# Another order for the attention's last seven tiles: 7, 0, 5, 1, 4, 2, 3 instead of 7, 5, 4, 3, 2, 1, 0

## The chip, the core and the metric

The kernel runs on one core of a Trainium2 chip. The metric is the device time of one execution in microseconds (us), the median over several runs. A core has a matrix engine (TensorE, PE in the profile), a vector engine (VectorE, DVE), an activation engine (ScalarE, ACT), a general engine (GpSimd, POOL) and a queue engine for transfers (SyncE, SP). Each runs its own instructions in order; they wait for one another through semaphores.

## The reference

The program is one inference step of a two-layer decoder trunk. Layer 0 mixes tokens by sparse attention, layer 1 by a recurrent block, and an expert mixer follows each. The change lies in layer 0's attention over the prompt of 2048 tokens:

```python
def block(args):                       # one block of Q_BLOCK = 128 queries
    qb, qib, wib, start = args
    q_pos = start + jnp.arange(Q_BLOCK)
    sc = indexer_scores(qib, wib, ki, q_pos, k_pos)     # causal
    _, idx = lax.top_k(sc, topk)                        # topk = 256
    valid = idx <= q_pos[None, :, None]
    return sparse_attend(qb, gather_rows(k, idx), gather_rows(v, idx), valid)
...
out = lax.map(block, (to_blocks(q), to_blocks(qi), to_blocks(wi), jnp.arange(nblk) * Q_BLOCK))
```

The 16 blocks don't depend on each other. There are 16 query heads and 4 key/value heads of 64 columns. The result goes through `attn_w_out`, is scaled by a gate and added to the input.

## The kernel before, in words

`phase_attend` (from L783) works through 16 **tiles** of 128 queries. Tile t sees the first 128(t + 1) keys, so its work grows with t. `TILE` (L848) lists the order; here "place m" is a position in that list and "tile t" the block of queries. The kernel doesn't gather keys. It computes all scores and hides those that were not chosen with a mask (`hide`). For tiles below `NPRE` = 9 the mask was made in an earlier phase and is loaded; for tiles 9 to 15 the indexer's work and the search run inside this phase.

All engines walk through the same stages: stage i works on the scores and values of place i and prepares the next places beside that. A stage has 2(t + 1) **slots** (`slots`, half of `S`), and `middle` is half of them. What a stage does in its slots:

- every slot: PE adds the mask and the maxima into two banks of PSUM (L1315), adds the scores by keys (L1322), and multiplies the two exponentials of the slot before by the values (L1333); ACT takes the exponentials (L1074);
- **first half** (slots below `middle`): the row maxima of the *next* place. PE fills a pair of scratch banks `aux` with scores in bf16 (L1342, `fill`), DVE takes the row maximum of each bank (L1166, `largest`). One pair of fills with its two maxima is a "pair" below; a next tile of up to 512 keys has 8 pairs, one of 513 to 1024 keys 16, of which every second covers the keys beyond 512. `fill` waits until the maximum that used the same bank is done. `unit_pairs_at` spreads the pairs evenly over the slots of the first half;
- first half too: DVE divides the *previous* place's output by its totals (`normalise`: four reciprocals at L1180 and one product at L1183), spread by `normal_at`, but all at once in slot 1 if `middle` is 2 or less;
- slot `middle`, after its own scores and values: PE projects the previous place's output (L1354, 32 matmuls), once the maxima of the next place (`maxed`) and the normalising (`o_normed`) are done;
- then ACT copies the projection (L1093) and the first half of this place's output (L1084), PE transposes the queries of place i + 2 (L1392), ACT copies them (L1120), and POOL adds the residual (L1040, L1043), sends it off (L1046) and narrows those queries to bf16 (L1051), which the next stage's `fill` needs.

So stages of neighbouring tiles are coupled: the number of pairs comes from the next tile, and the number of slots into which they go from this one:

```python
def unit_pairs_at(i, s):
    return share_of(U[i + 1] // 2, s, 0, max(middle(i), 1)) if there(i + 1) else range(0)
...
def normal_at(i, s):
    if middle(i) <= 2:
        return range(5) if s == min(1, middle(i)) else range(0)
    return share_of(5, s, 1, middle(i))
```

On PE a slot's order is: scores of this slot, the first half of its pairs, the values of the slot before, the other half of its pairs, and in slot `middle` the projection. When the last place is done, the phase ends with a barrier of all engines, and the sample group's phases follow.

Of the kernel before, what the change touches and what calls it, by code (L numbers as in the profile page):

```python
# [30 lines left out]
NT = SEQ // P  # L31
# [239 lines left out]
NPRE = 9  # L271
# [511 lines left out]
def phase_attend(nc, T):  # L783
# [7 lines left out]
    with ExitStack() as ctx, Semaphores(nc, T["whole_run"], ("y_out",)) as sems:  # L791
# [53 lines left out]
        hide_in = [sem("hide_in0"), sem("hide_in1")]  # L845

        RAMP = [6, 8]
        TILE = RAMP + [t for t in range(NT - 1, -1, -1) if t not in RAMP]  # L848
        L = [P * (t + 1) for t in TILE]
        CUTS = [-(-l // 512) for l in L]  # L850
        U = [H * c for c in CUTS]
        I = [0 if t < NPRE else IH * c for t, c in zip(TILE, CUTS)]
        S = [NKV * (t + 1) for t in TILE]
        PIECES = 37
# [5 lines left out]
        def there(m):  # L860
            return 0 <= m < NT

        def early(m):

            return there(m) and TILE[m] < NPRE

        def late(m):
            return there(m) and TILE[m] >= NPRE

# [97 lines left out]
        def rows_at(m):  # L967
            return slice(TILE[m] * P, TILE[m] * P + P)

# [2602 lines left out]
def build(nc, T):  # L3572
    with ExitStack() as stack:
# [8 lines left out]
        with ExitStack() as attention:  # L3582

            keep("KT", [P, NKV // 2, SEQ], until=attention)
            keep("kiT", [P, SEQ], until=attention)
            keep("V1", [P, NT, NKV, P], until=attention)
            with ExitStack() as projecting:
                keep("project_w", [P, KC, C_END], until=projecting)
                phase_modulation(nc, T)
                phase_project(nc, T)  # L3590
            phase_attend(nc, T)
# [81 lines left out]
```

## Time and profile before

| | us |
|---|---|
| median of 3 runs (5066.58 to 5074.35) | 5068.48 |
| the profiled execution: its time | 5068.78 |
| the profiled execution: its span | 5067.0 |
| PE busy, of the span | 4355.4 (86%) |
| DVE busy | 2225.7 (44%) |
| ACT busy | 1889.3 (37%) |
| POOL busy | 589.8 (12%) |

The span is what the profiler saw from the first instruction to the last; the time is 1.8 us more. The phase of the change runs from about 750 to 2480 us of it, its last seven tiles from 2076 us on.

### The profile page before, as it was taken

To read this page: it belongs to the slowest core of one execution; us is meant where nothing else is said; L and a number is where in the kernel's file an instruction comes from. 1 tells how busy PE (TensorE), PEld (TensorE's weight loads), DVE (VectorE), ACT (ScalarE), POOL (GpSimd) and SP (SyncE) were. 2 spreads that over 40 slices of the span, in tenths; PEclk is the share of its full clock that TensorE was granted. 3 is DMA by queue.
4 is the path that set the end of the run, shared out by engine and by line. 5 is a ranking of instruction groups with operands and counts; after the bars stand their busy time and mean duration, and the time that the engine had idled before them with its cause. 6 is when DMAs were issued, how large, how long until landed. Compare 5 with 4: busy or idle time off the path is not lost. (4 is left out here: it accounts for less than half of the span.)

```text
span 5067.0 us, 52791 instructions
## 1 busy us (share of the span) xinstructions
PE 4355.4 (86%) x15065; PEld 2214.0 (44%) x15067; DVE 2225.7 (44%) x5697; ACT 1889.3 (37%) x3264; POOL 589.8 (12%) x742
## 2 busy tenths in 40 slices
PE   7998876789999999998586699997999997699990
PEld 1544431223333333433334344444677775444440
DVE  1167875555655654233354211114566665411116
ACT  0134424766766663333122122222444443122223
POOL 0111111001011100112212000001000001100002
PEclk9999996889999999999886899997999998799995
DMA  8111111000000000000455777754121113467777
GB/s 303 51 50 45 38 37 53 11 7 15 9 15 15 13 15 15 28 27 21 155 179 218 296 278 282 264 195 149 52 71 67 67 38 123 154 237 284 285 263 283
DMA packets 152352, 596.45 MB, mean 118 GB/s; under 512 B 24303, under 2 KB 28271, under 8 KB 133176
## 3 DMA queue, kind: packets, MB, share of 16 engines
q1 hardware_dynamic: 99894, 424.39, 23.4%
q0 software_dynamic: 34208, 119.30, 6.8%
q10 hardware_dynamic: 18036, 50.22, 2.5%
q8 instruction: 97, 1.59, 0.1%
q14 instruction: 117, 0.96, 0.1%
HBM read 457.85 MB, written 136.06 MB: 117 GB/s over the span
## 5 line engine op out<-in xcount | busy, mean ns | idle before, releaser
L2728 PE MATMUL experts_ps_gu<-w_sb,experts_xT 128*128 x1504 | 679.3, 605 | 42.1 <-DMA w_sb<-moe_w_in 37.5
L1333 PE MATMUL attend_po<-attend_PT,V 128*128 128x512 f32 x1088 | 562.3, 638 | 23.5 <-ACT attend_total L1084 23.5
L763 PE MATMUL project_pj<-project_w,project_hT 128*128 128x424 f32 (+1 forms) x1360 | 510.7, 530 | 1.1 <-ACT project_hT L496 1.1
L3456 PE MATMUL recurrent_psAB<-recurrent_hT,rec_w_in_sb 128*128 128x256 f32 x2048 | 469.3, 383 | 0.8 <-ACT recurrent_hT L3122 0.8
L2728 PEld LDWEIGHTS experts_ps_gu<-w_sb,experts_xT 128*128 128x128 f32 x1504 | 285.0, 195 | 371.4 <-issue 371.4
L3456 PEld LDWEIGHTS recurrent_psAB<-recurrent_hT,rec_w_in_sb 128*128 128x128 f32 x2048 | 391.3, 192 | 68.8 <-issue 17.1
L1074 ACT ACTIVATE attend_PT<-attend_big 128x512 f32<-128x512 f32 x544 | 293.8, 592 | 329.8 <-PE attend_big L1322 328.9
L1111 ACT ACTIVATE attend_passed<-attend_score,attend_cand 128x2048 bf16<-128x2048 f32 (+6 forms) x217 | 365.5, 1684 | 100.5 <-DVE attend_cand L1224 82.5
L1166 DVE CUSTOM_DVE_ANT_0 attend_junk<-attend_aux,attend_hide 128x512 bf16<-128x512 f32 (+3 forms) x512 | 297.6, 620 | 195.4 <-issue 118.4
L2682 DVE SCALAR_TENSOR_TENSOR experts_th<-experts_th,experts_ps_gu 128x256 f32<-128x256 f32 x94 | 39.6, 422 | 747.1 <-ACT experts_th L2661 747.1
L763 PEld LDWEIGHTS project_pj<-project_w,project_hT 128*128 128x128 f32 (+1 forms) x1360 | 248.5, 187 | 245.0 <-issue 236.2
L2718 PE MATMUL experts_ps_y<-w_sb,experts_midT 128*128 x752 | 342.2, 598 | 11.5 <-issue 11.5
L1333 PEld LDWEIGHTS attend_po<-attend_PT,V 128*128 128x128 f32 x1088 | 188.2, 194 | 311.1 <-issue 248.9
L1322 PE MATMUL attend_big<-attend_qT,KT 64*128 64x512 f32 x1088 | 320.6, 667 | 0.0
L2661 ACT ACTIVATE experts_th<-experts_ps_gu 128x256 f32<-128x256 f32 x94 | 36.0, 383 | 677.9 <-PE experts_ps_gu L2728 677.9
L1342 PE MATMUL attend_aux<-attend_KTb,attend_qTb 64*128 64x512 bf16 (+3 forms) x640 | 171.3, 377 | 114.2 <-DVE attend_mx L1166 94.1
L1354 PE MATMUL attend_aux<-attend_w_out,attend_oT 128*128 128x512 f32 x512 | 225.8, 599 | 17.2 <-DVE attend_oT L1183 16.9
L3474 PE MATMUL recurrent_psO<-rec_w_out_sb,recurrent_yr 128*128 128x512 f32 x512 | 229.7, 592 | 0.0
L1342 PEld LDWEIGHTS attend_aux<-attend_KTb,attend_qTb 64*128 64x128 bf16 x640 | 47.1, 95 | 360.8 <-DVE attend_mx L1166 291.9
L2718 PEld LDWEIGHTS experts_ps_y<-w_sb,experts_midT 128*128 128x128 f32 x752 | 137.3, 193 | 149.0 <-issue 149.0
L2653 ACT ACTIVATE experts_y<-experts_ps_y 128x512 f32<-128x512 f32 x188 | 112.2, 597 | 187.7 <-PE experts_ps_y L2718 187.7
L1315 PE MATMUL attend_big<-attend_half_bias,attend_half_hide 128*128 128x256 bf16 x1088 | 172.3, 283 | 0.0
(597 smaller groups left out, 5684.1 us busy)
## 6 DMA issues: line engine op xcount, KB each, us to landing
w_sb<-moe_w_in SPq DMA_DIRECT2D x64, 2048.0 KB, 11.4
w_sb<-moe_w_in SPq DMA_DIRECT2D x64, 1024.0 KB, 8.4
yb_scratch<-experts_y ACTq DMA_DIRECT2D x94, 512.0 KB, 8.7
index_slab<-ada_w_in SPq DMA_DIRECT2D x12, 2048.0 KB, 9.7
yb_scratch<-route_blank SPq DMA_DIRECT2D x32, 512.0 KB
V<-ada_w_in SPq DMA_DIRECT2D x6, 2048.0 KB, 10.7
project_w<-attn_w_in_in SPq DMA_DIRECT2D x8, 1060.0 KB, 17.1
project_x<-x_prompt_in SPq DMA_DIRECT2D x16, 512.0 KB
```

Source lines behind the costliest of these rows:

```text
L763: last = pe.matmul(pj[0:rows, (t * NCH + c) % BANKS, 0:c1 - c0], hT[:, b, k, 0:rows], w[:, k, c0:c1], start=(k == 0), stop=(k == KC - 1))
L1074: act.activation(PT[:, g % 4, :], big[:, g % 4, :], ACT.Exp).then_inc(exped, 1)
L1111: act.activation(passed[:, 0:L[m]], score_of(m), ACT.Sign, bias=threshold, accum_out=balance[:, :]).then_inc(balanced, 1)
L1166: dve.tensor_tensor_reduce(junk[:, u % 2, 0:wide], aux[:, u % 2, 0:wide], hide_of(m)[:, keys], 1.0, LOWEST, ALU.add, ALU.max, mx[:, h, c:c ...
L1322: pe.matmul(big[:, g % 4, :], KT[r, n // 2, b * P:(b + 1) * P], qT[r, i % 3, n // 2 * GQ:(n // 2 + 1) * GQ, :].rearrange("p a q -> p (a q) ...
L1333: pe.matmul(po[:, n % 2, :], V1[:, b, n, :], PT[:, g % 4, :], start=(b == 0), stop=(b == S[i] // NKV - 1)).then_inc(pv_done, 1)
L1342: pe.matmul(aux[:, half, 0:keys.stop - keys.start], qTb[r, j * GQ + g, :], KTb[r, j, keys], start=True, stop=True).then_inc(unit_filled, 1)
L1354: last = pe.matmul(aux[:, half, :], oT[:, k, :], w_out[:, k, half * 512:half * 512 + 512], start=(k == 0), stop=(k == KC - 1))
L2718: last = pe.matmul(ps_y[:, half, :], midT[:, k, :], w2[:, bass.ds(slot, 1), k, half * 512:half * 512 + 512].rearrange("p a n -> p (a n)"), ...
L2728: last = pe.matmul(ps_gu[:, u, :], xT[:, u, k, :], w1[:, bass.ds(slot, 1), k, :].rearrange("p a n -> p (a n)"), start=(k == 0), stop=(k == ...
L3456: last = pe.matmul(psAB[:, part, 0:WB], w_in[:, k, part * D + c * P:part * D + (c + 1) * P], hT[:, n // KC % 2, k, :], start=(k == 0), sto ...
L3474: last = pe.matmul(psO[:, i * 2 + half, :], yr[:, n % 2, i * P:(i + 1) * P], w_out[:, c, half * 512:half * 512 + 512], start=(c == 0), sto ...
```

## The change

One list of seven numbers sets the order of the places 9 to 15. Places 0 to 8 (tiles 6, 8, 15, 14, 13, 12, 11, 10, 9) stay.

```diff
         RAMP = [6, 8]
-        TILE = RAMP + [t for t in range(NT - 1, -1, -1) if t not in RAMP]
+        FALL = [7, 0, 5, 1, 4, 2, 3]
+        TILE = RAMP + list(range(NT - 1, NPRE - 1, -1)) + FALL
         L = [P * (t + 1) for t in TILE]
         CUTS = [-(-l // 512) for l in L]
         U = [H * c for c in CUTS]
```

After the added line, every line of the changed kernel has a number higher by one (L1342 becomes L1343). The instructions of a tile stay the same; their neighbours change. Pairs of next tile and slots of this one, first halves only:

| stage of | next tile before: pairs into slots | next tile after: pairs into slots |
|---|---|---|
| tile 7 | 5: 16 into 8 | 0: 8 into 8 |
| tile 5 | 4: 16 into 6 | 1: 8 into 6 |
| tile 4 | 3: 8 into 5 | 2: 8 into 5 |
| tile 3 | 2: 8 into 4 | none |
| tile 2 | 1: 8 into 3 | 3: 8 into 3 |
| tile 1 | 0: 8 into 2 | 4: 16 into 2 |
| tile 0 | none | 5: 16 into 1 |

On PE, the matmuls that prepare tile 5 stood in the stage of tile 7. Before, the first slots of the stage behind tile 7 (the stage of tile 5, which prepares tile 4) read as follows; L1342 is a pair's fills, L1333 the values.

```order
L1322 MATMUL attend_big<-attend_qT,KT 128x512 x2
L1342 MATMUL attend_aux<-attend_KTb,attend_qTb 128x512 x2
L1333 MATMUL attend_po<-attend_PT,V 128x512 x2
L1342 MATMUL attend_aux<-attend_KTb,attend_qTb 128x128 x2
L1315 MATMUL attend_big<-attend_half_bias,attend_half_hide 128x4x64 x4
L1322 MATMUL attend_big<-attend_qT,KT 128x512 x2
L1342 MATMUL attend_aux<-attend_KTb,attend_qTb 128x512 x2
```

In the changed kernel the stage behind tile 7 is that of tile 0. Its slot 0 ends, after the values, with the second eight of sixteen pairs, and one slot later stands the projection:

```order
L1334 MATMUL attend_po<-attend_PT,V 128x512 x2
L1343 MATMUL attend_aux<-attend_KTb,attend_qTb 128x512 x2
L1343 MATMUL attend_aux<-attend_KTb,attend_qTb 128x256 x2
...
L1343 MATMUL attend_aux<-attend_KTb,attend_qTb 128x512 x2
L1343 MATMUL attend_aux<-attend_KTb,attend_qTb 128x256 x2
L1316 MATMUL attend_big<-attend_half_bias,attend_half_hide 128x4x64 x4
L1323 MATMUL attend_big<-attend_qT,KT 128x512 x2
L1334 MATMUL attend_po<-attend_PT,V 128x512 x2
L1355 MATMUL attend_aux<-attend_w_out,attend_oT 128x512 x16
```

A fill and a slot's scores no longer alternate there: eight pairs stand in a row before the values and eight behind them.

On DVE, before, the end of the stage of tile 5 has the maxima (ISA rows, each with the row that stores its result) between the parts of the normalising:

```order
L1180 RECIPROCAL attend_total<-attend_total 128x256
L1166 ISA attend_junk,attend_mx<-attend_aux,attend_hide_early 128x128
L1166 ISA attend_mx 128x1
L1166 ISA attend_junk,attend_mx<-attend_aux,attend_hide_early 128x128
L1166 ISA attend_mx 128x1
L1166 ISA attend_junk,attend_mx<-attend_aux,attend_hide_early 128x512
```

In the stage of tile 0 of the changed kernel the last maxima are followed by the reduction over them and the copies, and then by the whole normalising of tile 7's output:

```order
L1167 ISA attend_junk,attend_mx<-attend_aux,attend_hide_early 128x256
L1167 ISA attend_mx 128x1
L1171 TENSOR_REDUCE attend_negmax<-attend_mx 128x16
L1176 COPY attend_othermax<-attend_negmax 64x16 x2
L1181 RECIPROCAL attend_total<-attend_total 128x256 x4
L1184 TENSOR_TENSOR attend_oT<-attend_oT,attend_total 128x1024
```

The four reciprocals and the product have moved behind all sixteen pairs.

## Rows read from the trace of the kernel before

**Rows 1.** The head of the page.

```profile
span 5067.0 us, 52791 instructions
```

**Rows 2.** Windows: stages of tiles 7, 5, 4, 3, 2, 1, 0, slot 0 to projection.

```profile
2075.74:2111.00 35.26, 35.26 (x142) 13.66 (x141) 24.44 (x72) 12.79 (x26) 1.62 (x2) 1.00 0.02 5
2151.01:2184.52 33.51, 28.88 (x117) 11.35 (x116) 22.54 (x72) 10.62 (x22) 2.07 (x2) 1.00 0.01 4
2217.72:2242.60 24.88, 24.25 (x89) 9.03 (x88) 18.17 (x40) 9.51 (x20) 0.00 (x0) 1.00 0.00 1
2272.39:2293.28 20.89, 19.78 (x78) 7.65 (x77) 16.27 (x40) 8.45 (x18) 0.11 (x1) 1.00 0.00 1
2319.66:2344.92 25.26, 19.17 (x65) 7.08 (x64) 14.37 (x40) 7.36 (x16) 4.20 (x4) 0.86 0.00 1
2367.89:2389.70 21.81, 14.46 (x53) 5.70 (x52) 12.25 (x40) 6.61 (x15) 4.29 (x5) 0.84 0.04 14
2408.39:2422.40 14.01, 7.19 (x26) 2.59 (x24) 7.81 (x5) 5.20 (x13) 1.33 (x2) 0.87 0.22 75
```

**Rows 3.** Timeline of PE: a projection in tile 7's stage, then two slots.

```profile
2111.00 13.90 PE L1354 MATMUL attend_aux<-attend_w_out,attend_oT 128*128 128x512 f32 x32
2124.73 0.60 PE L1315 MATMUL attend_big<-attend_half_bias,attend_half_hide 128*128 128x256 bf16 x4
...
2130.55 0.60 PE L1315 MATMUL attend_big<-attend_half_bias,attend_half_hide 128*128 128x256 bf16 x4
...
2132.14 1.98 PE L1333 MATMUL attend_po<-attend_PT,V 128*128 128x512 f32 x4
2133.96 0.60 PE L1315 MATMUL attend_big<-attend_half_bias,attend_half_hide 128*128 128x256 bf16 x4
```

**Rows 4.** Timeline of PE: waits in the stages of tiles 1 and 0.

```profile
2383.73 0.50 PE L1342 MATMUL attend_aux<-attend_KTb,attend_qTb 64*128 64x128 bf16 x2 [5.87 <-DVE attend_mx L1166]
...
2422.40 15.53 PE L1354 MATMUL attend_aux<-attend_w_out,attend_oT 128*128 128x512 f32 x32 [6.82 <-DVE attend_oT L1183]
2440.17 1.10 PE L1333 MATMUL attend_po<-attend_PT,V 128*128 128x512 f32 x2 [2.25 <-ACT attend_total L1084]
...
2452.91 15.63 PE L1354 MATMUL attend_aux<-attend_w_out,attend_oT 128*128 128x512 f32 x32 [10.04 <-DVE attend_oT L1183]
```

**Rows 5.** Timeline of DVE: maxima 512, 256 and 128 wide; the copies behind them.

```profile
2153.01 0.69 DVE L1166 CUSTOM_DVE_ANT_0 attend_junk<-attend_aux,attend_hide_early 128x512 bf16<-128x512 f32 x1 [43.41 <-issue]
...
2153.62 0.69 DVE L1166 CUSTOM_DVE_ANT_0 attend_junk<-attend_aux,attend_hide_early 128x512 bf16<-128x512 f32 x1
...
2323.59 0.42 DVE L1166 CUSTOM_DVE_ANT_0 attend_junk<-attend_aux,attend_hide 128x256 bf16<-128x256 f32 x1 [1.27 <-PE attend_aux L1342]
...
2323.94 0.42 DVE L1166 CUSTOM_DVE_ANT_0 attend_junk<-attend_aux,attend_hide 128x256 bf16<-128x256 f32 x1
...
2384.73 0.29 DVE L1166 CUSTOM_DVE_ANT_0 attend_junk<-attend_aux,attend_hide_early 128x128 bf16<-128x128 f32 x1 [0.17 <-PE attend_aux L1342]
...
2384.95 0.29 DVE L1166 CUSTOM_DVE_ANT_0 attend_junk<-attend_aux,attend_hide_early 128x128 bf16<-128x128 f32 x1
...
2385.61 0.37 DVE L1175 COPY attend_othermax<-attend_negmax 64x16 f32<-64x16 f32 x2
```

**Rows 6.** Timeline of DVE: tile 6's pairs in one burst, one group apart.

```profile
776.98 0.69 DVE L1166 CUSTOM_DVE_ANT_0 attend_junk<-attend_aux,attend_hide_early 128x512 bf16<-128x512 f32 x1
...
779.54 0.69 DVE L1166 CUSTOM_DVE_ANT_0 attend_junk<-attend_aux,attend_hide_early 128x512 bf16<-128x512 f32 x1
```

**Rows 7.** Windows: the stretch with that burst.

```profile
750.00:800.00 50.00, 23.86 (x54) 6.97 (x57) 28.12 (x71) 4.87 (x6) 14.19 (x16) 0.50 0.40 138
```

**Rows 8.** Timeline of DVE: the normalising of tile 1's output.

```profile
2414.37 6.59 DVE L1180 RECIPROCAL attend_total<-attend_total 128x256 f32<-128x256 f32 x4 [28.39 <-ACT attend_total L1084]
2421.03 1.23 DVE L1183 TENSOR_TENSOR attend_oT<-attend_oT,attend_total 128x1024 f32<-128x1024 f32 x1
```

**Rows 9.** Timeline of POOL: queries narrowed after the projection of 2111.00.

```profile
2133.26 1.03 POOL L1051 CAST attend_qTb<-attend_qT 128x1024 bf16<-128x1024 f32 x1 [1.67 <-ACT attend_qT L1120]
```

## The prediction

> **What bounds the kernel now.** I read the windows of the seven last stages first, then PE's timeline through them, then its waits. The page gives a span of 5067.0 us [rows 1]. After this phase stands a barrier, and no later work starts before it, so what the phase gains or loses I carry one to one to the end.
>
> PE sets the pace while tiles are large. In tile 7's first half it is busy for all of 35.26 us at a granted clock of 1.00 [rows 2]; the columns are the length, the busy time of PE, of its weight loads, of DVE, ACT and POOL, and the clock. A plain slot, with no pairs in it, takes 2133.96 - 2130.55 = 3.41 us [rows 3]. A projection takes 2124.73 - 2111.00 = 13.73 us, and the slot after it 5.82 us, 2.41 more than a plain one, for the copy of the output banks and the turning of queries [rows 3]. Where no queries are turned only 1.54 is left: 2389.70 + 13.74 = 2403.44 to tile 0's slot 0 at 2408.39 is 4.95 us [rows 2].
>
> In small tiles PE waits for DVE. In tile 1's stage it stands 5.87 us before a fill, because the reciprocals stand between two maxima on DVE; then 6.82 us for tile 1's normalised output, 2.25 us for a copy, and 10.04 us at the very end [rows 4]. I take as a first half's **excess** its window less 3.41 us for each of its slots, the projection's included:
>
> | first half of tile | 7 | 5 | 4 | 3 | 2 | 1 | 0 |
> |---|---|---|---|---|---|---|---|
> | slots | 9 | 7 | 6 | 5 | 4 | 3 | 2 |
> | window | 35.26 | 33.51 | 24.88 | 20.89 | 25.26 | 21.81 | 14.01 |
> | excess | 4.57 | 9.64 | 4.42 | 3.84 | 11.62 | 11.58 | 7.19 |
>
> They sum to 52.9 us [rows 2]. Slots, projections and pairs are the same in number after the change; only excess and fixed costs move.
>
> **The prices on DVE.** A maximum starts 0.61 us after the one before at 512 keys, 0.35 at 256 and 0.22 at 128 [rows 5]. Sixteen pairs of tile 5 are eight groups of two 512 and two 256 wide maxima, 1.92 us each if DVE never waits; tile 4's groups (two 512, two 128) are 1.66. The one burst in the trace, tile 6's sixteen pairs, ran at 2.56 us a group of two 512 and two 384 wide ones [rows 6], because a fill can start only when its bank's maximum is done; its window has a granted clock of 0.50, the lower of the two levels throughout [rows 7]. I take 2.2 for tile 5 and 2.0 for tile 4, nearer the sum than the burst's row, since both are narrower. The normalising is 6.59 + 1.23 us, 7.9 with the gap between [rows 8]. From the start of the last maximum to the end of the last copy it is 2385.98 - 2384.95 = 1.03 us, of which 0.8 lies behind the maximum [rows 5].
>
> **The change, stage by stage.**
>
> *Tile 7* prepares tile 0: 8 narrow pairs in 8 slots. Its 16 mixed pairs cost 4.57, 0.29 each; at about 0.19 for a narrow one: 1.5.
>
> *Tile 0* prepares tile 5: all 16 pairs in slot 0, the normalising of tile 7 behind them, and then the projection. From slot 0 to DVE's first maximum 2.0 us (2151.01 to 2153.01) [rows 2, 5]. Then 8 x 2.2 = 17.6; in the middle PE multiplies the values for 1.98 us [rows 3] while DVE runs dry for about 1.5 of it; 0.8 for reduction and copies; 7.9; 0.14 to the projection. That is 29.9 us for two slots of 6.8: excess 23.1. ACT's copies of tile 7's output end some 12 us before DVE wants them and cost nothing; if they were late, all of it would shift. PE is behind DVE throughout, so its lower clock is hidden until the projection, which then runs as slowly as before (15.53 after a 6.82 us wait [rows 4]).
>
> *Tile 5* prepares tile 1: 8 pairs in 6 slots, about 3 us from tile 4's 4.42 and tile 3's 3.84. A new wait comes first. Tile 0 has no second half, so tile 1's queries are turned right behind the projection and wanted in the next slot. In the row they are narrowed 2133.26 - 2124.73 = 8.5 us after the projection's end and 1.03 us long, since POOL does the residual and its transfer first, and ACT the output's copies [rows 3, 9]. PE wants them at about 5.4 us; here ACT comes earlier to them and POOL is free at 6.9, so 8 us, and 2.4 us of wait. Behind the waiting fill stand this stage's slots. Excess 5.4.
>
> *Tile 1* prepares tile 4: 16 pairs in two slots and tile 5's whole normalising behind the first pair of slot 1. Slot 0: 2.0, four groups 8.0, gap 1.5, less the 0.4 by which PE's last fill precedes the maximum: 11.1. Slot 1: 2.0, one wide pair 1.2, normalising 7.9, one narrow pair 0.4, three groups 6.0, gap 1.5, less 0.5: 18.5. Slot 2: 3.4 at full clock, at most twice that at half; I take 3.9. In all 33.5 for 10.2: excess 23.3. Tile 1's before was 11.58, with half as many and narrower pairs.
>
> *Tile 4* prepares tile 2: 8 pairs, 384 wide: between the two rows of 8 pairs, 4.1.
>
> *Tile 2* prepares tile 3: 8 pairs of 512 instead of 256. Each maximum is 0.26 longer, and of 16 some 8 lie in the chain behind the reciprocals: 11.62 + 2.2 = 13.8.
>
> *Tile 3*, last, prepares nothing and has 3 slots to hide tile 2's normalising: 0. Tile 0's 6.82 us wait is gone with this.
>
> Sum: 1.5 + 23.1 + 5.4 + 23.3 + 4.1 + 13.8 + 0 = 71.2, so +18.3. Fixed costs: the turning happens five times as before, but the copy behind a projection is paid in front of further slots once more, +1.5. At the end, PE has nothing between the last slot and ACT's copies, but no 2.25 us wait and little of the second copy: 14.98 us (2452.91 less the end of the projection of 2422.40, 15.53 later) becomes about 12.4: -2.6. In all **+17.3**, on 5068.78 us for the profiled execution (0.3 above the median): 5086.
>
> The bounds: with groups at 1.92 and 1.66 and no gap for the values, tile 0 is 3.8 lower and tile 1 5.4; with tile 2 and tile 5 also as cheap as they can be (-2.2, -1.5) the change costs 4 us. With groups at 2.56, tile 0 is 2.9 higher, tile 1 3.9; a slow projection in tile 1's stage adds 1.8, tile 5 and tile 2 2 each, a halved clock in slot 2 about 3: +33.
>
> The Trainium skill ("VectorE: DVE Perf Modes", First, the fixed hardware budget) says that a reciprocal is divided iteratively, with a repeat count of 8. By that and the page's 0.96 GHz, an estimate for four of 256 columns is 8.5 us, where the row has 6.59: the stages of tiles 0 and 1 would each be 1.9 us longer and the sum +21. The measurement decides, and I keep 6.59.
>
> **Rivals.**
>
> *The bursts overlap better than I count* (0.13). PE's scores and values fill DVE's time and groups run at the sum. For it: narrow pairs need short fills. Against: the burst row, 2.56. Then 4 to 10 us: 5073 to 5078.
>
> *Not slower* (0.04). What the old order exposes at the end (6.82, 2.25) counts, and what the small stages prepare doesn't: a pair costs its 0.29 of PE, DVE keeping step. Stages 0 and 1 would each be 16 x 0.29 + 7.9 = 12.5 excess, tile 2 as before 11.6, the others as above: 47.1, so -5.8 + 1.5 - 2.6 = -6.9: 5062. It decides if a group takes no more than 4 x 0.15 us on DVE; the rows have 1.66 at least, so I give it little. Beyond -0.2% tile 2's excess would have to fall too.
>
> *The clock stays low* (0.09). Through both bursts PE computes little. In tile 2's, 1's and 0's first halves the granted clock was 0.86, 0.84 and 0.87, a mixture of 2.4 and 1.2 GHz, and 0.50, thus 1.2 alone, around the burst at the start [rows 2, 7]. If fills run at 1.2 GHz throughout and the work behind starts so, the upper prices hold: 5098 to 5104. The Trainium skill ("TensorE: Matmul & The Clock Gate", HAM oscillation) warns of just this, that idle gaps make PE start each burst at half clock. By that rule, the trace agrees.
>
> *As forecast* (0.74): 5078 to 5098.
>
> **The numbers.** A measurement of this kernel can tell about 0.2%, 10 us, from nothing. Slower by more than that is the forecast, the low clock and a little of the first rival: 0.84. Within 0.2% (up to 5078.6): 0.14. Faster: 0.02. The range leaves about one in ten on each side: 5073, inside the first rival, to 5101, inside the low clock's.
>
> **What the profile would show.** The projection behind tile 0's two slots starts some 30 us after slot 0, waiting for the product of the normalising, with sixteen pairs in a row on DVE and one break for the values. The fill of tile 1's pairs waits some 2 us for POOL. Tile 1's first half takes 33 us, with an 8 us wait before its second fill of slot 1. Tile 3's has no wait. The last projection follows its last values by some 12 us. The prediction is wrong if groups are far from 2 us, or if ACT's or POOL's queue is late for a cause I priced at nothing: the mask's loading, or the diagonal of the maxima, which POOL makes in 4 us behind tile 0's pairs while PE projects.

## The result, and the profile after

The changed kernel takes 5104.01 us (median of 5 runs, 5093.0 to 5111.33), the kernel before 5074.35 on the same chip (median of 5, 5066.58 to 5081.84). The ratio is 1.0062, 95% interval 1.0046 to 1.0079: slower by 0.6%. The prediction had the direction and 17 us of the 30; the time lies 3 us above its range. Part of that distance is the base: the forecast stood on 5068.48 us, the median of three runs. Three single executions among those used below lie far out, one of the kernel before (5262.65 us) and two of e2 (8980.06 and 20799.4 us), for a cause that the record doesn't show; the ratios leave them out, and a ratio on record can differ from that of the two medians by up to 0.1%. The profiled execution took 5093.0 us. Its page begins:

```profile
span 5091.3 us, 52791 instructions
```

Because a whole execution scatters by some 10 us to each side, at times by 20, I compare the **stretch** from tile 7's slot 0 to the end of the last projection. Before it is 2452.91 + 15.63 - 2075.74 = 392.80 us [rows 2, 4]; after, 2491.29 + 15.86 - 2083.92 = 423.23 us, so +30.4. The rest of the program holds nothing of the change. PE's timeline has the last row of the stretch:

```profile
2491.29 15.86 PE L1355 MATMUL attend_aux<-attend_w_out,attend_oT 128*128 128x512 f32 x32 [10.44 <-DVE attend_oT L1184]
```

The windows of the seven first halves after the change, in the order 7, 0, 5, 1, 4, 2, 3, answer to [rows 2]. The columns are the same:

```profile
2083.92:2116.75 32.83, 32.83 (x125) 12.51 (x124) 12.49 (x40) 12.77 (x26) 1.90 (x1) 1.00 0.01 3
2156.77:2189.11 32.34, 22.77 (x58) 6.68 (x56) 24.95 (x72) 5.19 (x12) 4.17 (x3) 0.72 0.02 5
2207.65:2237.83 30.18, 27.74 (x103) 10.46 (x101) 14.09 (x40) 14.69 (x31) 7.21 (x7) 0.94 0.17 56
2271.02:2312.17 41.15, 25.41 (x69) 8.51 (x68) 22.73 (x72) 6.28 (x14) 3.71 (x3) 0.67 0.01 3
2331.73:2355.97 24.24, 23.71 (x90) 8.94 (x88) 16.18 (x40) 11.78 (x24) 2.72 (x5) 1.00 0.21 66
2385.76:2414.12 28.36, 21.50 (x65) 7.55 (x64) 18.45 (x40) 7.37 (x16) 3.16 (x2) 0.82 0.00 0
2436.22:2453.47 17.25, 17.25 (x62) 6.86 (x61) 7.81 (x5) 8.43 (x18) 0.00 (x0) 1.00 0.08 33
```

The two stages with a burst of sixteen pairs stand out twice: they are long, and their granted clock is 0.72 and 0.67, between the two levels (1.00 is 2.4 GHz throughout, 0.50 is 1.2 GHz throughout). The excess (window less 3.41 us a slot), beside the forecast and an experiment that comes below:

| first half of tile | 7 | 0 | 5 | 1 | 4 | 2 | 3 | sum |
|---|---|---|---|---|---|---|---|---|
| before | 4.57 | 7.19 | 9.64 | 11.58 | 4.42 | 11.62 | 3.84 | 52.9 |
| forecast | 1.5 | 23.1 | 5.4 | 23.3 | 4.1 | 13.8 | 0 | 71.2 |
| after | 2.14 | 25.52 | 6.31 | 30.92 | 3.78 | 14.72 | 0.20 | 83.6 |
| after, clock kept up (e5) | 2.15 | 23.03 | 6.15 | 23.69 | 3.78 | 13.96 | 0.20 | 73.0 |

Tile 1 alone has 7.6 us of the 12.4 by which the sum was missed, tile 0 has 2.4.

**Inside tile 0's first half.** PE's timeline: the last fill of the first burst, the values, the first fill behind them, then slot 1's scores and values, the projection, and two rows of tile 5's stage:

```profile
2166.76 0.39 PE L1343 MATMUL attend_aux<-attend_KTb,attend_qTb 64*128 64x256 bf16 x1 [0.22 <-DVE attend_mx L1167]
2167.09 3.78 PE L1334 MATMUL attend_po<-attend_PT,V 128*128 128x512 f32 x4
2170.80 0.39 PE L1343 MATMUL attend_aux<-attend_KTb,attend_qTb 64*128 64x512 bf16 x2
...
2180.73 2.08 PE L1323 MATMUL attend_big<-attend_qT,KT 64*128 64x512 f32 x4
2182.74 2.83 PE L1334 MATMUL attend_po<-attend_PT,V 128*128 128x512 f32 x4
2189.11 16.75 PE L1355 MATMUL attend_aux<-attend_w_out,attend_oT 128*128 128x512 f32 x32 [3.54 <-DVE attend_oT L1184]
...
2213.66 0.28 PE L1343 MATMUL attend_aux<-attend_KTb,attend_qTb 64*128 64x256 bf16 x2 [2.44 <-POOL attend_qTb L1052]
...
2215.70 3.41 PE L1334 MATMUL attend_po<-attend_PT,V 128*128 128x512 f32 x4
```

The same four matmuls of the values that took 1.98 us in [rows 3] take 3.78 here, and behind the 2.44 us wait for POOL again 3.41. DVE's timeline shows what that costs in the middle of the burst:

```profile
2158.76 0.69 DVE L1167 CUSTOM_DVE_ANT_0 attend_junk<-attend_aux,attend_hide_early 128x512 bf16<-128x512 f32 x1 [42.77 <-PE attend_aux L1343]
...
2171.22 0.69 DVE L1167 CUSTOM_DVE_ANT_0 attend_junk<-attend_aux,attend_hide_early 128x512 bf16<-128x512 f32 x1 [3.60 <-PE attend_aux L1343]
...
2181.07 6.59 DVE L1181 RECIPROCAL attend_total<-attend_total 128x256 f32<-128x256 f32 x4
2187.73 1.22 DVE L1184 TENSOR_TENSOR attend_oT<-attend_oT,attend_total 128x1024 f32<-128x1024 f32 x1
```

DVE is dry for 3.60 us where I had taken 1.5. DVE's maxima come in **groups** of two wide and two narrow ones (two pairs). The four groups ahead of the gap took 2171.22 - 2158.76 - 3.60 = 8.86, 2.2 us each, as forecast. Windows of three pieces of this half tell when the clock went. The third piece is the values alone:

```profile
2156.77:2162.27 5.50, 3.49 (x16) 1.16 (x15) 3.46 (x13) 1.08 (x2) 0.39 (x1) 1.00 0.00 0
2162.27:2167.09 4.82, 3.57 (x10) 0.88 (x10) 4.38 (x18) 0.00 (x0) 0.00 (x0) 0.68 0.01 2
2167.09:2170.80 3.71, 3.71 (x5) 1.17 (x6) 0.43 (x2) 1.51 (x4) 0.00 (x0) 0.50 0.00 0
```

PE never stood still for more than 0.88 us in there. It did short fills with waits of 0.2 to 0.9 us between them, and by the time of the values the granted clock was 0.50, the lower level of 1.2 GHz.

**Inside tile 1's first half** the same happens three times. PE, then DVE:

```profile
2276.55 3.68 PE L1334 MATMUL attend_po<-attend_PT,V 128*128 128x512 f32 x4
...
2284.17 1.04 PE L1316 MATMUL attend_big<-attend_half_bias,attend_half_hide 128*128 128x256 bf16 x4
...
2297.05 0.81 PE L1343 MATMUL attend_aux<-attend_KTb,attend_qTb 64*128 64x512 bf16 x2 [7.72 <-DVE attend_mx L1167]
...
2299.27 3.78 PE L1334 MATMUL attend_po<-attend_PT,V 128*128 128x512 f32 x4
...
2307.97 2.08 PE L1323 MATMUL attend_big<-attend_qT,KT 64*128 64x512 f32 x4
2309.98 2.36 PE L1334 MATMUL attend_po<-attend_PT,V 128*128 128x512 f32 x4
```

```profile
2280.58 0.69 DVE L1167 CUSTOM_DVE_ANT_0 attend_junk<-attend_aux,attend_hide_early 128x512 bf16<-128x512 f32 x1 [3.63 <-PE attend_aux L1343]
...
2287.67 0.69 DVE L1167 CUSTOM_DVE_ANT_0 attend_junk<-attend_aux,attend_hide_early 128x512 bf16<-128x512 f32 x1 [3.10 <-PE attend_aux L1343]
...
2303.63 0.69 DVE L1167 CUSTOM_DVE_ANT_0 attend_junk<-attend_aux,attend_hide_early 128x512 bf16<-128x512 f32 x1 [3.95 <-PE attend_aux L1343]
```

The second gap is the one between slot 0 and slot 1, where PE adds the mask (L1316) and the scores: 2287.67 - 2284.17 = 3.5 us from slot 1's start to DVE's first maximum, where I had 2.0.

### The profile page after: what moved, and what is told of

The parts are those of the page before. It is cut to its first block and busy times, and to the rows that moved or that the text cites. A ratio compares the mean times of both kernels' runs of the same rounds, so it can differ in the third digit from the quotient of the medians.

```text
span 5091.3 us, 52791 instructions
## 1 busy us (share of the span) xinstructions
PE 4389.4 (86%) x15065; PEld 2219.9 (44%) x15067; DVE 2226.2 (44%) x5697; ACT 1889.3 (37%) x3264; POOL 588.3 (12%) x742
## 5 line engine op out<-in xcount | busy, mean ns | idle before, releaser
L3457 PEld LDWEIGHTS recurrent_psAB<-recurrent_hT,rec_w_in_sb 128*128 128x128 f32 x2048 | 388.2, 191 | 67.6 <-issue 17.2
L1167 DVE CUSTOM_DVE_ANT_0 attend_junk<-attend_aux,attend_hide 128x512 bf16<-128x512 f32 (+3 forms) x496 | 283.0, 610 | 194.5 <-PE attend_aux L1343 113.9
L1343 PE MATMUL attend_aux<-attend_KTb,attend_qTb 64*128 64x512 bf16 (+3 forms) x640 | 179.9, 385 | 123.9 <-DVE attend_mx L1167 103.4
L1343 PEld LDWEIGHTS attend_aux<-attend_KTb,attend_qTb 64*128 64x128 bf16 x640 | 48.0, 95 | 377.9 <-DVE attend_mx L1167 298.5
L1316 PE MATMUL attend_big<-attend_half_bias,attend_half_hide 128*128 128x256 bf16 x1088 | 174.2, 285 | 0.0
## 6 DMA issues: line engine op xcount, KB each, us to landing
project_w<-attn_w_in_in SPq DMA_DIRECT2D x8, 1060.0 KB, 17.3
```

The costliest lines, as they stand in the source:

```text
L1167: dve.tensor_tensor_reduce(junk[:, u % 2, 0:wide], aux[:, u % 2, 0:wide], hide_of(m)[:, keys], 1.0, LOWEST, ALU.add, ALU.max, mx[:, h, c:c ...
L1343: pe.matmul(aux[:, half, 0:keys.stop - keys.start], qTb[r, j * GQ + g, :], KTb[r, j, keys], start=True, stop=True).then_inc(unit_filled, 1)
L3457: last = pe.matmul(psAB[:, part, 0:WB], w_in[:, k, part * D + c * P:part * D + (c + 1) * P], hT[:, n // KC % 2, k, :], start=(k == 0), sto ...
```

## The experiments

"Stretch" is that of the profiled execution; before it is 392.80 us, after 423.23. Ratios are to the kernel before on the same chip.

**e1: the changed kernel again.** No edit.

> The changed kernel as it is, once more, to see what a second profile and more runs say. In the first pair of profiles the stretch from tile 7's slot 0 to the end of the last projection grew from 392.8 to 423.2 us (+30.4), while the work ahead of it was 8.2 us longer and the work behind it 14 us shorter. Theory A: the stretch is the change's own cost and the rest is scatter between executions. Then the stretch is again 422 to 424 us, the total ratio 1.005 to 1.007, and the parts ahead and behind differ from before by other amounts. Theory B: the order also speeds up later phases by some 14 us. Then the part behind, from the end of the last projection to the end of the span, is again about 2584 us, as against 2598 before.

5105.14 us (5096.98 to 5118.5, 6 runs) against 5070.33; ratio 1.0072 (1.0053 to 1.0091). Its stretch is 423.22 us, the first one's 423.23. What stands ahead of it took 2072.8 us in one profiled execution and 2083.9 in the other, what stands behind 2605.9 and 2584.2. So the scatter of the total lies outside, and here the stretch repeated to 0.01 us. That is two executions of one kernel; e9 below shows a projection that differs by 1.7 us between two runs though the 47 us ahead of it are equal, so a difference of 2 us between stretches can be that.

**e2: only tile 0 early.**

```diff
-        FALL = [7, 0, 5, 1, 4, 2, 3]
+        FALL = [7, 0, 5, 4, 3, 2, 1]
```

> One part of the change alone: tile 0 behind tile 7, the others falling (7, 0, 5, 4, 3, 2, 1). If the cost is that of the bursts, each by itself: tile 0's first half takes 32 us as in the changed kernel (excess 25.5) and its projection 16.7; tile 5's has a wait of 2.4 us for the queries; tile 1 as last has only its normalising in two slots (excess 3.5). Sum of excesses 64 against 52.9, the ending 2.7 cheaper: +10 us in all. If what costs is the alternation as a whole (every stage next to one of another size), it would be near half of the 30, +15 or more, spread over tiles 5 and 4 too.

5088.71 us, ratio 1.0036 (1.0022 to 1.0049); stretch 408.58, +15.8. Tile 0's first half is 32.33 us, as in the full change. Tile 5's excess is 16.4 instead of 9.64: it now stands behind tile 0, which has no second half. Two rows of PE:

```profile
2180.74 16.73 PE L1355 MATMUL attend_aux<-attend_w_out,attend_oT 128*128 128x512 f32 x32 [3.57 <-DVE attend_oT L1184]
...
2205.26 0.61 PE L1343 MATMUL attend_aux<-attend_KTb,attend_qTb 64*128 64x512 bf16 x2 [4.35 <-POOL attend_qTb L1052]
```

The fill waits 4.35 us for POOL. I had expected +10, and had named +15 or more, spread over tiles 5 and 4, as the sign that the alternation costs as a whole. The number is the second one, but the spread isn't there: tile 4's excess is 4.42 as before. What I had missed is tile 5 (6.8 us more than before, with a longer wait for POOL than the 2.4 I took) and the projections, together 4 us above those before. The price of a small tile placed early is paid in its own stage, in its projection (16.73 for 13.90) and in the stage behind it.

**e3: only tile 1 early.**

```diff
-        FALL = [7, 0, 5, 1, 4, 2, 3]
+        FALL = [7, 5, 1, 4, 3, 2, 0]
```

> The other part alone: tile 1 between tiles 5 and 4, the others falling (7, 5, 1, 4, 3, 2, 0). Burst theory: tile 1's first half takes 41 us (excess 30.9) as in the changed kernel; tile 2 prepares tile 0, excess about 9.5; tile 0 last as before, 7.2. Sum 63 against 52.9: +10 us. Had tile 1 been slow only because tile 0's stage shortly before left the clock low, its first half would be some 35 us and the total +4.

5083.75 us, ratio 1.0025 (1.0012 to 1.0038); stretch 402.32, +9.5. Tile 1's excess is 31.4 (after: 30.9), tile 5's falls to 2.15 with narrow pairs, tile 2's to 8.58. Tile 0's stage doesn't stand ahead of it here, so tile 1 isn't slow because that stage left the clock low. Its excess follows from its own slots and pairs; tile 5's depends on what stands before it too (e2). 15.8 and 9.5 make 25 of the 30.4. The rest lies in stages that have other neighbours in each order: tile 2 has 14.7 in the full change but 10.1 in e2 and 8.6 in e3, and tile 1 as the last stage has only 3.8 in e2; tiles 3 and 5 go the other way.

**e4: idle matmuls in the two stages.** **Idle matmuls**, whose result is overwritten by the next scores, stand behind every pair, ahead of the long wait and ahead of tile 0's projection. Nothing of the computation is left out.

```diff
+                def spin(i, s, n, wide=384):
+                    g = sum(S[:i]) + 2 * s + 2
+                    pe.wait_ge(exped, g + 1)
+                    keep_running(pe, big[:, g % 4, 0:wide], identb[:, 0, :], KTb[:, 0, 0:wide], n)
...
                         for u in units[:len(units) // 2]:
                             fill(i + 1, u)
+                            if warmed(i):
+                                spin(i, s, 2 if u != units[1] or s == 0 else 36)
...
+                            if warmed(i):
+                                spin(i, s, 2)
...
+                                if warmed(i) and middle(i) == 1:
+                                    spin(i, s, 30)
                                 project(i - 1)
```

> The changed kernel, with idle matmuls of 384 columns on PE in the stages of tiles 0 and 1: two behind each pair, 36 more before the long wait in tile 1's slot 1, 30 before the projection in tile 0's stage. They write a bank of scores that the next slot overwrites; nothing else is changed. Theory A (the burst's cost beyond the forecast is the halved clock): the granted clock of both first halves rises from 0.72 and 0.67 to above 0.95, the values between two bursts take 2.0 instead of 3.8 us, tile 0's projection 13.9 instead of 16.75. Tile 0's first half falls from 32.3 to about 30, tile 1's from 41.2 to about 34, in all 11 to 13 us less than the changed kernel. Theory B (DVE sets the pace whatever the clock, and the dry stretches come from queueing on PE): both first halves stay or get longer by what the added matmuls take, and the total is within 3 us of the changed kernel or above it.

5097.56 us, ratio 1.0057 (1.0038 to 1.0075); stretch 415.63, 7.6 less than after. Tile 1 fell from 41.15 to 37.56 us, tile 5 from 30.18 to 28.54 and tile 0's projection from 16.75 to 13.90, but tile 0 rose from 32.34 to 33.35. The idle matmuls themselves were in the way: two between narrow fills make a group longer (the first narrow fills of two groups that follow each other start at 2151.95 and 2154.38, 2.4 us apart for 2.2), and the thirty reach to the very start of the projection. DVE's product had ended at 2181.28, so the projection started about 1.1 us late:

```profile
2160.40 1.88 PE L1334 MATMUL attend_po<-attend_PT,V 128*128 128x512 f32 x4
...
2177.67 5.04 PE L260 MATMUL attend_big<-attend_KTb,attend_identb 128*128 128x384 bf16 x30
2182.54 13.90 PE L1363 MATMUL attend_aux<-attend_w_out,attend_oT 128*128 128x512 f32 x32
```

**e5: fewer of them, better placed.** Three behind each pair of 512 keys and none behind a narrow one, 44 ahead of the long wait, 24 ahead of tile 0's projection.

```diff
                         for u in units[:len(units) // 2]:
                             fill(i + 1, u)
+                            if warmed(i) and u == units[1] and s == 1:
+                                spin(i, s, 44)
+                            elif warmed(i) and unit_pair(i + 1, u)[2] == 0:
+                                spin(i, s, 3)
...
```

> The changed kernel with idle matmuls as in e4, but placed so that they delay no fill and no projection: 3 behind each pair whose keys reach 512 columns or more in the stages of tiles 0 and 1, 44 ahead of tile 1's long wait for the pair behind the reciprocals, and 24 ahead of tile 0's projection. They write to score banks that the next scores overwrite, so the output stays. The low-clock theory: values between the bursts fall from 3.78 to about 2 us in all three places, groups stay at 2.0 to 2.3 us, tile 0's first half falls from 32.3 to about 30.3 us and tile 1's from 41.2 to about 35.5; the stretch of the seven tiles falls from 423.2 to 411 or 412 us. The rival, that the bursts are held by DVE alone and the clock is only a symptom: tile 0 and tile 1 stay at 32 and 41 us or grow by what the idle matmuls delay.

5092.05 us against 5069.74, ratio 1.0034 (1.0012 to 1.0055); stretch **409.70**, 13.5 less than after. The windows of tile 0's first half, its projection, and tile 1's first half have a granted clock of 1.00:

```profile
2154.21:2184.06 29.85, 24.95 (x105) 9.42 (x104) 25.11 (x72) 5.19 (x12) 4.17 (x3) 1.00 0.02 6
2184.06:2198.03 13.97, 13.97 (x32) 5.98 (x32) 0.00 (x0) 0.60 (x1) 0.00 (x0) 1.00 0.00 0
2263.05:2296.97 33.92, 29.80 (x138) 12.55 (x136) 22.73 (x72) 6.28 (x14) 2.12 (x3) 1.00 0.02 4
```

Values of tile 0 and tile 1 on PE, with the 44 idle matmuls between, then DVE's gaps behind the values:

```profile
2164.35 1.98 PE L1334 MATMUL attend_po<-attend_PT,V 128*128 128x512 f32 x4
...
2268.57 1.98 PE L1334 MATMUL attend_po<-attend_PT,V 128*128 128x512 f32 x4
...
2277.88 7.32 PE L260 MATMUL attend_big<-attend_KTb,attend_identb 128*128 128x384 bf16 x44
...
2287.68 1.99 PE L1334 MATMUL attend_po<-attend_PT,V 128*128 128x512 f32 x4
```

```profile
2166.69 0.69 DVE L1167 CUSTOM_DVE_ANT_0 attend_junk<-attend_aux,attend_hide_early 128x512 bf16<-128x512 f32 x1 [1.80 <-PE attend_aux L1351]
...
2270.91 0.69 DVE L1167 CUSTOM_DVE_ANT_0 attend_junk<-attend_aux,attend_hide_early 128x512 bf16<-128x512 f32 x1 [1.94 <-PE attend_aux L1351]
```

The prediction had 29.9 us for tile 0 and 33.5 for tile 1, and its stretch was 392.8 + 17.3 = 410.1. These two stages come to that at full clock; the stages of tiles 5 and 2 still have 0.94 and 0.88. Of the 13.5 us, tile 1's half gave 7.2, tile 0's projection 2.8, its half 2.5 and tile 2's half 0.8. The groups hardly moved: (2166.69 - 2156.20 - 1.80) / 4 = 2.2 us, 2156.20 being DVE's first maximum there. The theory of the low clock holds. The rival, that DVE alone accounts for what the bursts cost beyond the forecast, falls: added work on PE made them shorter.

**e6: the division behind the slot's maxima, after the change.** In stages with a middle slot of 2 or less.

```diff
-                            if n == 0 and there(i - 1):
+                            if n == 0 and there(i - 1) and not (i > 9 and middle(i) <= 2):
                                 for part in normal_at(i, s):
                                     normalise(i - 1, part)
...
+                        if i > 9 and middle(i) <= 2 and there(i - 1):
+                            for part in normal_at(i, s):
+                                normalise(i - 1, part)
```

> The changed kernel, but in stages with a middle slot of 2 or less DVE divides the previous output behind the slot's maxima and no longer behind its first pair. If the 7.7 us wait before tile 1's second fill of slot 1 costs what stands behind it, tile 1's first half falls by some 5 us, from 41.2 to about 36: the fills of slot 1 and the values now run while nothing is pending, and the reciprocals' 7.9 us lie behind the last maximum, partly beside slot 2's scores and values; a wait of about 4 us stands before the projection instead. Tile 0 does not change (its normalising is behind the pairs already), and neither do tiles 7, 5 and 4. Tile 2 changes by a few us either way. Rival: the division is on the path wherever it stands, and tile 1 stays within 1 us of 41.

One run of 5112.75 us, so without an interval; the stretch is 422.85, 0.4 less than after. Tile 1's first half fell from 41.15 to 37.78 us, not by 5, and the gain came back behind it:

```profile
2309.47 16.58 PE L1358 MATMUL attend_aux<-attend_w_out,attend_oT 128*128 128x512 f32 x32 [3.65 <-DVE attend_oT L1184]
```

After the change this projection had no wait and took 13.90 us. The wait moved from the fill to the projection, which then took 2.7 us more; tile 2's half was 0.7 longer.

**e7: the same edit in the kernel before, in all stages from place 10 on.**

```diff
-                            if n == 0 and there(i - 1):
+                            if n == 0 and there(i - 1) and not (i > 9):
```

> The kernel before, with DVE's parts of the normalising behind each slot's maxima instead of between its first and second pair, from place 10 on. The 5.87 us wait before tile 1's second fill and the similar one in tile 2's stage go; the waits before the projections grow by 1 to 3 us. Stretch of the seven tiles 3 to 6 us shorter than 392.8; total about 5064 to 5067, not to be told from before with certainty. Rival: the division is on the path wherever it stands, no difference of stretch.

5066.32 us (12 runs) against 5069.74, ratio 0.9994 (0.9981 to 1.0008); stretch 389.19, -3.6. Tile 5 gains 1.5 us, tile 2 4.3 and tile 1 1.7; tiles 4 and 3, where the old place was hidden, lose 1.0 and 1.3. That is -5.2 in excess; 1.5 came back in tile 1's projection (15.44 for 13.90).

**e8: tile 0 ahead of tile 1 at the end.**

```diff
-        FALL = [7, 0, 5, 1, 4, 2, 3]
+        FALL = [7, 5, 4, 3, 2, 0, 1]
```

> Order 7, 5, 4, 3, 2, 0, 1 instead of 7, 5, 4, 3, 2, 1, 0: tile 2 prepares tile 0 (8 narrow pairs into 3 slots), tile 0 prepares tile 1 (8 pairs of 256 keys into slot 0), and tile 1, last, prepares nothing and hides tile 0's normalising in part. Bursts of narrow pairs: excess of tile 2 about 8.6 as where it prepared a narrow tile in e3, tile 0 about 14 (8 pairs in one slot and 7.9 us of normalising, values once at half clock), tile 1 about 3.8. Sum of these three 26 to 27 against 30.4 before, so the stretch is about 4 us shorter than 392.8, total 5064 to 5070. If every burst beside a small tile costs as tile 0's and 1's did after the change (25 and 31 us), tile 0 alone would have 20 us and more and the stretch would be longer than before.

5074.48 us (12 runs) against 5069.74, ratio 1.0007 (0.9992 to 1.0022); stretch 388.57, -4.2. Excess of tile 2 8.4, of tile 0 12.0, of tile 1 5.9 (expected 8.6, 14 and 3.8). The total shows nothing of the 4 us, which is at the edge of its interval. So it is not a small tile ahead of others that costs, but sixteen wide pairs put into it: eight narrow ones in one slot cost half as much.

**e9: the late division only where it gained.**

```diff
-                            if n == 0 and there(i - 1) and not (i > 9):
+                            if n == 0 and there(i - 1) and not (i > 9 and middle(i) in (2, 3, 6)):
```

> The kernel before, with the normalising behind each slot's maxima only in the stages where e7 gained by it: those of tiles 5 (-1.5 us), 2 (-4.3) and 1 (-1.7). The stages of tiles 4 and 3, where it cost 1.0 and 1.3 us, keep their old place. Stretch of the seven tiles 392.8 - 7.5 = 385.3, if the stages' excesses do not depend on one another; the total then about 0.15% below before, at the edge of what can be told. Rival: what a stage gains comes back as a wait in the next one, and the stretch stays near e7's 389.2.

5069.15 us (12 runs) against 5071.08, ratio 0.9996 (0.9982 to 1.001); stretch 389.03, where I had expected 385.3. The excess fell by 7.5 as expected, 52.9 to 45.4. But the projections behind tiles 2 and 1 took 15.67 and 15.77 us for 13.90 each, which is the missing 3.6. The first of the two is a surprise beside e7. There the same projection stands behind the same wait, and the 47 us ahead of it hold the same 141 matmuls at the same distances, with a granted clock of 1.00 in both. The row of e7, then that of e9:

```profile
2341.57 13.97 PE L1357 MATMUL attend_aux<-attend_w_out,attend_oT 128*128 128x512 f32 x32 [3.04 <-DVE attend_oT L1183]
2344.10 15.67 PE L1357 MATMUL attend_aux<-attend_w_out,attend_oT 128*128 128x512 f32 x32 [3.04 <-DVE attend_oT L1183]
```

So a wait of 3 us may or may not bring the clock down for the work behind it, and no run here shows what decides it. e7's stretch owes 1.7 us to it.

**e10: e9 in the order of e8.** Both edits together.

> e9 in the order of e8 (7, 5, 4, 3, 2, 0, 1). Tile 5's stage -1.5 us as in e7; tile 2's (tile 0's narrow pairs in 3 slots, division behind them) 8.4 less about 2; tile 0's as in e8, 12.0, since its normalising is behind the pairs already; tile 1's, last, prepares nothing: 5.9. Stretch 388.6 - 3.5 = about 385, the same as e9: the two gains are in part the same one. Total 0.1 to 0.2% below before. Rival: the gains add in full, and the stretch is 381 us.

5066.7 us (12 runs) against 5071.08, ratio 0.9982 (0.9969 to 0.9995); stretch 387.75, -5.1, where I had 385. Tile 0's half had an excess of 13.4 for the 12.0 of e8. Windows of its last four projections:

```profile
2344.24:2359.91 15.67, 15.67 (x34) 6.80 (x35) 0.00 (x0) 0.60 (x1) 0.00 (x0) 0.89 0.00 0
2389.24:2404.90 15.66, 15.66 (x34) 6.80 (x35) 0.00 (x0) 0.60 (x1) 0.00 (x0) 0.89 0.00 0
2420.88:2436.47 15.59, 15.59 (x34) 6.87 (x35) 0.00 (x0) 0.60 (x1) 0.00 (x0) 0.90 0.00 1
2453.59:2469.88 16.29, 16.29 (x32) 6.90 (x32) 0.00 (x0) 0.60 (x1) 0.00 (x0) 0.86 0.00 0
```

**e11: e10 with idle matmuls in the waits ahead of these four.**

```diff
+                IDLE = {13: 12, 14: 20, 15: 14, 16: 56}
...
                             if there(i - 1):
+                                spin(i, s)
                                 project(i - 1)
```

> e10 with idle matmuls (384 columns, their results overwritten) ahead of the last four projections, which there wait 2.91, 4.25, 3.41 and 10.45 us for the division and then take 15.7, 15.7, 15.6 and 16.3 us instead of 13.9: 12, 20, 14 and 56 of them, 0.17 us each at full clock, which fills each wait but for about 1 us. If what the late division gave back is the clock that falls in those waits, the four projections take 13.9 us each again, the stretch falls by about 7 us from 387.8 to 381 and the total stands about 0.3% below before. If idle matmuls don't help there, or end later than the division, the stretch stays at 387 or more.

5058.95 us (12 runs) against 5070.3, ratio 0.9983 (0.9969 to 0.9997); stretch **378.93**, 13.9 less than before and 44.3 less than after. Windows of two of the projections, the other two being alike:

```profile
2334.45:2348.42 13.97, 13.97 (x34) 6.21 (x35) 0.00 (x0) 0.60 (x1) 0.00 (x0) 1.00 0.00 0
...
2437.31:2451.28 13.97, 13.97 (x32) 5.96 (x32) 0.00 (x0) 0.60 (x1) 0.00 (x0) 1.00 0.00 0
```

The four fell by 63.21 - 55.88 = 7.3 us, and tile 0's first half by 1.5 more: the values in its middle took 1.98 us for 3.31, and DVE's gap there 1.70 us for 3.02. Its stretch is the shortest of all here. Its total can't be told from e10's, whose ratio is 0.9982; the interval of either excludes 1, but by little.

## Why the prediction was right and where it was wrong

**Right: what the change does.** Sixteen pairs in slot 0 of tile 0 and sixteen in two slots of tile 1 make DVE the pace there, the projection waits for the division, and the large stages gain little. Groups were forecast at 2.2 and 2.0 us and measured at 2.2 and 2.0 (tile 1's first group runs from 2273.02 to 2275.02). The division with its gaps was forecast at 7.9 us and runs from 2181.07 to the projection at 2189.11, 8.0. The Trainium skill ("VectorE: DVE Perf Modes", First, the fixed hardware budget) gives a repeat count of 8 for a reciprocal, from which the estimate was 8.5 us for the four alone; the row after the change has 6.59 again. The wait for POOL was forecast at 2.4 us and is 2.44. Excesses of tile 4, tile 3, tile 7 and tile 2 came within 1 us each.

**Near by the experiments, in part by luck.** With the clock kept up (e5) the stretch is 409.70 us against a forecast of 410.1. The terms are less close than the sum. The excess is 73.0 against 71.2, so 1.8 more; the fixed costs are -3.2 against -1.1, so 2.1 less, of which 1.6 is tile 0's projection, which I had left at its slow 15.53 us and which took 13.97. The two misses cancel. (Two slips of mine are small: the terms of the sum give +17.2, and those of the rival "not slower" an excess of 47.6 for the 47.1 that I wrote.)

**Wrong: the clock in the bursts.** The step that failed reads: "PE is behind DVE throughout, so its lower clock is hidden until the projection", together with the price of 1.5 us for the time that DVE is dry while PE multiplies the values. What the runs showed in its place: PE's lower clock is hidden only while PE's work lies beside DVE's. At four places the two alternate: each time values or scores stand between two fills, DVE's queue is empty, and all of PE's time is on the path, at half speed. I priced these with a row from a stage at full clock [rows 3]. Term by term:

| term | forecast | after | e5 |
|---|---|---|---|
| tile 0, gap for the values | 1.5 | 3.60 | 1.80 |
| tile 1, gap for the values in slot 0 | 1.5 | 3.63 | 1.94 |
| tile 1, slot 1's start to DVE's first maximum | 2.0 | 3.50 | 1.92 |
| tile 1, gap for the values in slot 1 | 1.5 | 3.95 | 1.93 |
| tile 1, slot 2 | 3.9 | 5.01 | 3.42 |
| tile 0's projection | 15.53 | 16.75 | 13.97 |

These are 2.1 + 2.1 + 1.5 + 2.45 + 1.1 + 1.2 = 10.5 us of the 13.1 by which the stretch was missed (30.4 - 17.3). Not all of it is the clock: at full clock the three gaps for the values are 1.80 to 1.94 us, so 0.3 to 0.4 of each was priced too low in any case. The rest is small: tile 5 0.9, whose values behind the wait for POOL ran at half clock too, tile 2 0.9, tile 7 0.6, the fill behind tile 1's division 0.6, less terms of the other sign. That the low clock was the cause and not a companion is shown by e5: only idle matmuls were added, and 13.5 us went.

**The rivals.** The time came out at the upper edge of the low clock's (5098 to 5104), to which I gave 0.09. As a difference it is at the lower one: +30.4 on the 5068.5 us that I started from is 5099, which would have been inside my range. So that the time fell outside it is in part scatter of the base, and the number alone doesn't decide; the rows do. That rival's mechanism was half right: the groups did not go to 2.56 us, since DVE covers the fills even at half clock. What grew was what stands between bursts. I also had the evidence: the burst of tile 6 had a granted clock of 0.50 [rows 7], and a price of 1.98 us for PE's four matmuls of the values was read at 1.00; at 0.50 they take 3.78. The Trainium skill ("TensorE: Matmul & The Clock Gate", A second HAM failure mode: psum-queue depth-cycling) describes this pattern, PE idling briefly between groups of matmuls often enough that the clock swings. By that rule, the trace agrees: the granted clock was 0.72 and 0.67 in the two stages, with no wait above 0.88 us in tile 0's burst. "Not slower" is excluded by the measured +30.4, and "the bursts overlap better" by the groups, which ran at 2.2 us and not at their sum of 1.92.

**What stays open.** e11 keeps its clock and stands 13.9 us below before in the stretch; its total stands 11.4 us below in the medians, with an interval of 0.03% to 0.31%. What decides whether the clock falls in a wait of some 3 us is open (e7 against e9). How many idle matmuls are enough was not tried, nor was e5's edit joined to e11's. Nor do I know why what stands ahead of and behind the stretch varies between executions: over the profiled ones from 2072.3 to 2084.9 us ahead, from 2582.1 to 2609.3 behind.

## What to carry to other kernels

When two engines alternate on the path, price each at the speed it will have there, not at that of a busy stage: look up the granted clock of the nearest stretch with the same pattern, and count every place where the work does not overlap. A reordered chain moves a wait, and the wait itself can have a price behind it. Of the projections behind a wait of 2.9 to 4.3 us here, one (e7's) took no more than at full clock, and the others 1.7 us more, or 2.7 to 2.9 behind a half with a granted clock of 0.72 or less. That ate some 30% of e7's gain, half of e9's and most of e6's, until idle matmuls filled the waits (e11). And a stage of few slots should not get the wide preparation of its neighbour; eight narrow pairs beside tile 0 cost 12 us of excess, sixteen mixed ones 25.5.

## What the runs showed of the hardware that was not expected

- The granted clock fell to the lower level without any long wait: fills of 0.3 to 1.5 us with waits of 0.2 to 0.9 us between them took it from 1.00 to 0.68 and then 0.50 in tile 0's first burst.
- It fell late: in e10 the projection behind a 2.91 us wait starts out of a first half with a granted clock of 1.00, and has 0.89 itself. The price of a wait lies in the work behind it. It isn't paid each time: in e7 a projection behind 3.04 us kept 1.00, in e9 the same one behind the same wait had 0.89.
- Idle matmuls in place of short waits held it at 1.00 (e5, e11), three of 384 columns a pair (0.66 us) being enough here. Where they made groups longer and ran past the end of the wait (e4), 7.6 us were gained for 13.5.
- The stretch repeated to 0.01 us in a second execution, while the total differed by 11 us (after and e1).
